# Causal prompt attention: one score product per softmax map, the mask added on VectorE

## What is computed

```python
def diff_attn_core(q, qpos, segs, lam):
    """q: (B,Q,H,2,DK); segs: [(k (B,K,H,2,DK), v (B,K,H,DV), kpos (K,))] -> (B,Q,H,DV) f32."""
    scale = DA_DK ** -0.5
    for k, v, kpos in segs:
        s = jnp.einsum('bqhcd,bkhcd->bhcqk', q, k).astype(jnp.float32) * scale
        scores.append(jnp.where(kpos[None, :] <= qpos[:, None], s, NEG))
    p = jax.nn.softmax(jnp.concatenate(scores, axis=-1), axis=-1)
    a = p[:, :, 0] - lam * p[:, :, 1]
    ...
        outs.append(jnp.einsum('bhqk,bkhd->bqhd', a[..., off:off + nk], v.astype(jnp.float32)))
```

## Time and profile before

| | |
|---|---|
| median of 3 runs | 2162.46 us |
| the profiled execution, its own time | 2167.23 us |
| its span, first to last instruction | 2165.6 us |
| mean granted TensorE clock | 0.938 |
| TensorE busy | 1924.2 us (89%), 11596 instructions |
| DVE busy | 581.3 us (27%) |
| ACT busy | 506.7 us (23%) |

### The profile page before, as it was taken

The page is one execution under the profiler, slowest core; times in us unless marked ns, Lnnn a source line. Parts: engine busy times, 40 slices in busy tenths (PEclk is TensorE's granted clock), DMA queues, the critical chain, the costliest instruction groups (busy, mean ns, idle before and its releaser), DMA issues. The chain is left out here.

```text
span 2165.6 us, 30574 instructions
## 1 busy us (share of the span) xinstructions
PE 1924.2 (89%) x11596; PEld 1143.2 (53%) x11596; DVE 581.3 (27%) x1571; ACT 506.7 (23%) x1072; POOL 181.8 (8%) x236
## 2 busy tenths in 40 slices
PE   7999988888979999999499998897889799999970
PEld 3467766555454445454245777564645445445430
DVE  3113336421133111110420333743112411111003
ACT  2122326545110001011111222554521001001001
POOL 1000013110000000000100000401000000000002
PEclk9999989999888999999699999999989799999985
DMA  8320038889623988986522101888982378988743
GB/s 286 118 87 22 1 111 278 293 281 338 227 100 129 332 325 303 332 316 232 209 82 77 40 14 46 281 285 277 328 300 109 115 268 300 332 323 306 285 146 143
DMA packets 209282, 453.26 MB, mean 209 GB/s; under 512 B 23217, under 2 KB 23218, under 8 KB 209138
## 3 DMA queue, kind: packets, MB, share of 16 engines
q1 hardware_dynamic: 189986, 383.52, 51.1%
q0 software_dynamic: 19152, 67.77, 8.3%
HBM read 413.89 MB, written 37.36 MB: 208 GB/s over the span
## 5 line engine op out<-in xcount | busy, mean ns | idle before, releaser
L914 PE MATMUL bank<-wslots,heads 128*128 128x512 f32 x768 | 339.5, 599 | 2.7 <-DVE heads L1627 2.7
L620 PE MATMUL bank<-xT,wslots 128*128 128x272 f32 x1024 | 241.4, 393 | 1.5 <-ACT heads L1174 0.8
L914 PEld LDWEIGHTS bank<-wslots,heads 128*128 128x128 f32 x768 | 146.3, 192 | 182.3 <-issue 178.8
L620 PEld LDWEIGHTS bank<-xT,wslots 128*128 128x128 f32 x1024 | 191.5, 190 | 40.2 <-issue 3.2
L574 PE MATMUL bank<-wslots,xT 128*128 128x512 f32 x384 | 173.7, 608 | 0.0
L666 PE MATMUL bank<-cst,wslots 128*128 128x128 f32 x1024 | 165.6, 290 | 9.2 <-ACT wslots L1224 3.0
L1753 DVE SCALAR_TENSOR_TENSOR temps<-temps,smalls,bank 128x512 f32<-128x512 f32 x32 | 23.9, 748 | 432.4 <-PE bank L914 432.4
L666 PEld LDWEIGHTS bank<-cst,wslots 128*128 128x128 f32 x1024 | 117.6, 146 | 35.8 <-issue 25.2
L574 PEld LDWEIGHTS bank<-wslots,xT 128*128 128x128 f32 x384 | 73.1, 195 | 90.2 <-issue 90.0
L866 PE MATMUL bank<-wslots,xT 128*128 128x512 f32 x256 | 116.1, 615 | 3.8 <-DVE xT L1526 3.8
L935 PE MATMUL bank<-wslots,temps 128*128 128x512 f32 x256 | 112.7, 593 | 1.5 <-ACT temps L1266 1.5
(11 more groups left out here) (335 smaller groups left out, 2148.4 us busy)
## 6 DMA issues: line engine op xcount, KB each, us to landing
wslots<-in_w_up SPq DMA_DIRECT2D x33, 2048.0 KB, 21.1
wslots<-in_cache_k SPq DMA_DIRECT2D x256, 256.0 KB, 4.3
wslots<-in_cache_v SPq DMA_DIRECT2D x256, 256.0 KB, 4.3
wslots<-in_w_gate SPq DMA_DIRECT2D x17, 2048.0 KB, 16.3
hgrn<-in_w_down SPq DMA_DIRECT2D x17, 2048.0 KB, 10.6
hgrn<-in_w_gate SPq DMA_DIRECT2D x16, 2048.0 KB, 16.4
wslots<-in_w_down SPq DMA_DIRECT2D x16, 2048.0 KB, 10.5
wslots<-in_w_in SPq DMA_DIRECT2D x14, 2048.0 KB, 9.8
```

The lines of the kernel that those rows point to most:

```text
L620: x = mm(bank[6 + g % 2][:, 0:HALF], w[:, c, h * P:(h + 1) * P], xT[:, c, half * HALF:(half + 1) * HALF], start=(c == 0), stop=(c == DC - 1))
L914: x = mm(bank[2 + k][:, :], xeT[e % 2][:, c, :], w[:, c, :], start=(c == 0), stop=(c == DC - 1))
```

## The change

`scores` issues one product per map over all (i + 1) key blocks, diagonal included, and no mask product. VectorE, ahead of the maximum, adds `cmask` in place to the diagonal block of both maps, in PSUM, and waits for that.

```diff
@@ -627,13 +627,8 @@
                 if U >= 2:
                     pe.wait_ge(pa_exp, U - 1)
                 for c in range(2):
-                    o = bank[c + 2 * (u % 2)]
                     a, z = 64 * c, 64 * (c + 1)
-                    q = qT[a:z, h, tok(i)]
-                    if i > 0:
-                        mm(o[:, 0:i * P], q, kT[a:z, h, 0:i * P], start=True, stop=True)
-                    mm(o[:, i * P:(i + 1) * P], q, kT[a:z, h, tok(i)], start=True, stop=False)
-                    x = mm(o[:, i * P:(i + 1) * P], ident, con("cmask"), start=False, stop=True)
+                    x = mm(bank[c + 2 * (u % 2)][:, 0:(i + 1) * P], qT[a:z, h, tok(i)], kT[a:z, h, 0:(i + 1) * P], start=True, stop=True)
                 x.then_inc(pa_qk, 1)
 
             def turn_a(l, u):
@@ -1660,6 +1655,10 @@
                         w = (u // H + 1) * P
                         dve.wait_ge(pa_qk, U + 1)
                         for c in range(2):
+                            o = bank[c + 2 * (u % 2)][:, tok(u // H)]
+                            x = V.tensor_tensor(o, o, con("cmask"), ALU.add)
+                        link(x)
+                        for c in range(2):
                             x = V.tensor_reduce(mx[:, u % 2, c:c + 1], bank[c + 2 * (u % 2)][:, 0:w], AX, ALU.max)
                         link(x)
                         link(V.tensor_scalar(mx[:, u % 2, :], mx[:, u % 2, :], -1.0, None, ALU.mult), pa_max)
```

## The result

The changed kernel takes 2115.8 us (median of 4 runs, 2108.49 to 2118.04), the kernel before 2162.3 us beside it. The ratio is 0.9779 with a 95% interval of 0.9763 to 0.9796, a gain of 44 to 51 us; the forecast was 44.0 us and 2118.5 us. A second set of 5 runs gave 0.9781 (0.9758 to 0.9804).

A forecast was written before the change was run, and what follows sets the result against it. TensorE, busy throughout both attention-score stages, was taken as the bound. Mask products, form changes and full map overlap save 44.0 us: 2167.2 - 44.0 = 2123.2 profiled, less 4.8 for the median, 2118.5 us; range 2113 to 2138.

The forecast's parts named there:

- (1): TensorE score blocks: two mask products and two 0.20 us changes of array form go, 0.83 us per unit, 27 us.
- (2): Both maps' score products, on separate halves of the array rows, run at the same time: 44.0 us with (1); chance 0.68.
- Partial overlap: Rival: of the maps' passes, started strictly in order, only the middle two overlap; 36 us saved, 2126.5 us; chance 0.10.
- no overlap: Rival: the two maps' products run one behind the other; 27 us saved, 2135.5 us; chance 0.16.
- (3): DVE's two mask additions per unit, ahead of the maximum: 0.5 to 0.75 us, taken as 0.5, covered, costed at nothing.
- The room of 3.0 us: Unit 13's turn, last query block: mix ends at 247.03 with the shorter block; TensorE wants it at 248.72; additions take 0.5 to 0.75.
- (4): SP and POOL queues keep the same instructions; cache-page transfers behind the stage start earlier along with it; no size given.
- absorbed: Rival: a transfer that does not move ends last behind the stage; gain goes, within 0.2% of 2162; chance 0.04.
- The rival on the slower side: Mask additions delay maximum and mix, so TensorE waits; gain lost at 4.4 us per pair, 2182 us at 5; chance 0.02.

## Why the prediction was right, point by point

- TensorE bounds the stage, and what it no longer does the stage no longer lasts: right. It is busy 100.43 of 100.43 us before and 77.63 of 77.63 after, and the stage becomes 45.6 us shorter where 44.0 were forecast.
- (1), the change of form, 0.20 us each way: right on the way in. The Trainium skill, "TensorEngine Tiling (Array Packing)", section "Key Properties", says that a change of tiling mode drains the engine; the rows agree, with 0.10 us of gap and 0.10 us of open weight load. On the way out it was over-sized for 28 of the 32 units, where a transpose follows: 0.06 us instead of 0.10, which with the rounding of the blocks is the 1.6 us between 44.0 and 45.6.
- (2), the overlap, the one unknown: right as taken, full. The trace shows it, and the run with a wait between the maps takes it away and loses 27.3 us, 17 of them overlap. Partial overlap fell with the blocks (0.42 us measured, 0.52 forecast for it), and no overlap too (0.63). The Trainium skill, "TensorE: Matmul & The Clock Gate", section "Part 3: Packing small matmuls — row/col tiling", has 3.07x for four row tiles; the estimate worked out from it, 39 us, was too low.
- (3), DVE's pair: 0.50 us as taken, and costs nothing, also when it is tripled. The room of 3.0 us was right for one mix (0.5 used, 2.5 left).
- (4), nothing else moves: nothing was absorbed, since in both profiles of the change the stretches behind did not grow; they are some us shorter than before, which is left open above. One thing did move: TensorE's waits for cache pages in the whole run, 2.1 us before, are 7.5 and 5.3 us in these two profiles. They are 4.7 to 5.5 us in the other runs too, also with seven pairs, where the stage is no shorter than before, so they do not follow the gain.
- The rival on the slower side was priced wrongly. It reckoned only the way from scores to mix, and so a pair of 4.4 us before the gain is lost. Seven pairs, 3.7 us, lose it already: DVE's turn of 2.9 to 4.1 us, the pair in it, becomes the bound with 1.4 to 1.8 us of further additions, since TensorE's turns have shrunk to 4.3 to 5.9 (worked out from the turns; the run with 1.1 us more is free, the one with 3.2 us more is not). That step was missing; it did not matter at 0.50 us.

## To carry over

Where TensorE works on products of several array forms, count the changes of form: two neighbours that use different halves of the array rows and write different banks cost here as much as one, and a small product of another form between them costs two changes and the overlap. Work moved to an engine off the critical path is free as long as that engine's whole turn stays under the turn of the engine that sets the pace, which the change has just made shorter; the way of one item through it is only half of the test.

## What the runs showed of the hardware

Two float32 products on separate halves of the array rows overlap completely here (1.05 us for the pair at 512 columns, 2.24 with a wait between them), though both write all 128 partitions, of two banks. They do so too when another product of the first half stands between them in the program (1.07 us for 384 and 128 columns each). The decode stage differs by up to 10 us between executions of kernels that do not differ in it, one profile each, while the two profiles of the change agree to 0.8 us; what sets that was not tried.
